# Short-convolution units regrouped between the chunks of a 31-tap convolution, with layer norm pieces and input statistics moved, in an eight-core Conformer block

## The reference

```
sh1, sc1, gt1, sh2, sc2, gt2 = split(silu(c) @ w_ada + b_ada, 6)
h = rmsnorm(x, norm1_g) * (1 + sc1) + sh1
p = h @ w_in                          # 2*512 + 3*512 + 2*1024 columns
# mixer A
u = (u_a + b) * sigmoid(u_b + b)
u = causal_dwconv(u, width 31) + conf_dw_b
u = silu(layernorm(u))
y_a = u @ conf_w_out + conf_b_out
# mixer B
v = g_b * causal_dwconv(g_c * v, width 3)
y_b = v @ sc_w_out
mixed = (sigmoid(g1) * y_a + sigmoid(g2) * y_b) @ w_o
x = x + gt1 * mixed
h2 = rmsnorm(x, norm2_g) * (1 + sc2) + sh2
x = x + gt2 * ((silu(h2 @ w_g) * (h2 @ w_u)) @ w_down)
out = rmsnorm(x, final_g)
```

## Time and profile before

| | us |
|---|---|
| median of 3 runs | 923.08 |
| the profiled execution | 923.02 |
| its span on core 2, the slowest | 921.5 |
| span of the other cores | 918.5 to 921.4 |
| TensorE busy | 874.9 |
| VectorE busy | 470.6 |
| ScalarE busy | 325.1 |
| POOL busy | 28.9 |

### The profile page before, as it was taken

One profiled execution on the slowest core, in us unless ns is written; L12 is line 12 of the kernel. 1 busy time (PEld: TensorE's weight loads), 2 busy tenths in 40 slices (PEclk: granted clock), 3 DMA queues, 4 the chain that ended last, 5 costly groups with the idle time before them and its releaser, 6 DMA issues.

```text
span 921.5 us, 13134 instructions; the slowest of 8 cores (918.5 to 921.5 us)
## 1 busy us (share of the span) xinstructions
PE 874.9 (95%) x4487; PEld 402.6 (44%) x4487; DVE 470.6 (51%) x741; ACT 325.1 (35%) x496; POOL 28.9 (3%) x58
## 2 busy tenths in 40 slices
PE   3698899899999999999999999999999999999995
PEld 0243344444444444444444444444444444444464
DVE  2767846666666666657742212472213532214677
ACT  4676776655522222237751111101110011112333
POOL 0000000000000000000110000000000000000000
PEclk9999999999999999999999999999999999999998
DMA  8995444671658736294008212231222222101225
GB/s 233 291 261 139 94 105 103 136 145 31 173 125 256 193 97 156 70 196 124 1 1 138 35 35 46 46 55 27 35 46 46 47 35 35 35 9 27 91 104 172
DMA packets 29155, 91.93 MB, mean 100 GB/s; under 512 B 3233, under 2 KB 13729, under 8 KB 24866
## 3 DMA queue, kind: packets, MB, share of 16 engines
q1 hardware_dynamic: 23618, 59.26, 21.8%
q0 software_dynamic: 5184, 31.57, 20.5%
q10 hardware_dynamic: 288, 0.26, 0.1%
HBM read 105.73 MB, written 8.39 MB: 124 GB/s over the span
## 4 chain that ended last, share of the span: by engine, by line
PE 82%; DVE 6%; ACT 4%; issue 3%; DMA 3%; SPq 1%; DVEq 0%; ACTq 0%
PE ps L363 62%; PE ps L1098 17%; DVE arena L345 4%; ACT arena L342 3%; DMA arena<-xc 2%; DVE arena L349 2%; PE ps L773 2%; PE ps L655 1%; SPq L413 1%; ACT L342 1%; PE ps L560 1%; PE ps L453 0%; DMA arena<-arena 0%; DVE arena L352 0%; DMA outT<-arena 0%
## 5 line engine op out<-in xcount | busy, mean ns | idle before, releaser
L363 PE MATMUL ps<-arena 128*128 128x512 bf16 (+1 forms) x3028 | 661.7, 380 | 10.8 <-DVE arena L345 5.1
L363 PEld LDWEIGHTS ps<-arena 128*128 128x128 bf16 (+1 forms) x3028 | 296.1, 98 | 370.5 <-issue 18.0
L345 DVE TENSOR_TENSOR arena<-ps,arena 128x512 bf16<-128x512 f32 (+2 forms) x158 | 108.1, 685 | 305.8 <-PE ps L363 221.9
L342 ACT ACTIVATE arena<-arena 128x512 bf16<-128x512 f32 (+3 forms) x233 | 149.6, 673 | 145.8 <-DVE arena L349 77.5
L342 ACT ACTIVATE arena<-ps 128x512 f32<-128x512 f32 x122 | 71.9, 594 | 303.4 <-PE ps L363 302.7
L349 DVE SCALAR_TENSOR_TENSOR arena<-ps,arena 128x512 f32<-128x512 f32 (+2 forms) x176 | 127.4, 725 | 69.7 <-PE ps L1098 41.1
L1098 PE MATMUL ps<-arena 128*128 128x512 bf16 (+1 forms) x800 | 154.0, 353 | 0.0
L345 DVE TENSOR_TENSOR arena<-arena 128x512 f32<-128x512 f32 (+5 forms) x211 | 125.7, 619 | 36.7 <-ACT arena L342 23.5
L342 ACT ACTIVATE arena<-ps,arena 128x512 f32<-128x512 f32 (+1 forms) x117 | 76.4, 686 | 122.3 <-PE ps L363 105.8
L1098 PEld LDWEIGHTS ps<-arena 128*128 128x128 bf16 x800 | 78.3, 98 | 74.2
L349 DVE SCALAR_TENSOR_TENSOR arena<-arena 128x512 f32<-128x512 f32 (+3 forms) x83 | 57.6, 703 | 21.5 <-ACT arena L342 17.4
(11 more groups left out here) (25 smaller groups left out, 33.8 us busy)
## 6 DMA issues: line engine op xcount, KB each, us to landing
arena<-wada SPq DMA_DIRECT2D x48, 512.0 KB, 7.8
arena<-w POOLq DMA_DIRECT2D x21, 1024.0 KB, 9.6
arena<-arena SPq DMA_DIRECT2D x64, 130.0 KB, 2.8
arena<-xc SPq DMA_DIRECT2D x8, 1024.0 KB, 8.2
arena<-xc SPq DMA_DIRECT2D x4, 2048.0 KB, 17.3
arena<-wd POOLq DMA_DIRECT2D x8, 768.0 KB, 6.9
outT<-arena SPq DMA_DIRECT2D x24, 256.0 KB, 2.9
arena<-w POOLq DMA_DIRECT2D x6, 512.0 KB, 11.5
```

Source lines behind the costliest of these rows:

```text
L342: sch.op("act", lambda e: e.activation(out=out, in_=in_, func=func, **kw), reads=reads, writes=writes)
L345: sch.op(eng, lambda e: e.tensor_tensor(out=out, in0=in0, in1=in1, op=op), reads=reads, writes=writes)
L363: fns.append(lambda e, lt=lt, rh=rh, i=i: e.matmul(bank[b], lhsT=lt, rhs=rh, start=(i == 0), stop=(i == n - 1)))
```

## The change

Six things are changed, all in `stages`:

1. `in_tmp(1, ·)` is called for two tiles each at k = 1, 2, 3 and 4, in place of four at k = 1 and four at k = 2.
2. `in_sq(2)` moves from behind unit (0,1) to behind unit (0,0). The hook with `in_red(2, 6)` and `in_apply(2)` moves from ahead of the third group of unit (1,0) to ahead of its second. `glu_raw(2, 0)` moves ahead of unit (1,0).
3. In `in_apply` the h tile k = 7 is written by VectorE and no longer by ScalarE.
4. In the u units after chunk 0 both `st_a` and `st_b` are issued behind u(1,3), and `st_j` for j = 0 and 1 behind u(2,3) and u(3,3).
5. Chunk 1 follows after unit (0,2). Between chunks 1 and 2, and between 2 and 3, there are four units, and three after chunk 3. The statistics and pieces fill the first three units after each chunk.
6. The empty piece before the layer norm of chunk 3 goes, and a function `warm` that nothing called.

```diff
-            def warm(n):
-                sch.pe_group([lambda e: e.matmul(bank[0][:, 0:416], lhsT=ones_d, rhs=cst, start=True, stop=True) for _ in range(n)],
-                             reads=[B_cst], writes=[B_bank[0]])
...
-                if k == 1:
-                    for kk in range(4):
-                        in_tmp(1, kk)
-                elif k == 2:
-                    for kk in range(4, KD):
-                        in_tmp(1, kk)
+                for kk in {1: (0, 1), 2: (2, 3), 3: (4, 5), 4: (6, 7)}.get(k, ()):
+                    in_tmp(1, kk)
...
                 for k in ks:
                     in_tmp(r, k)
-                    in_h(r, k, "act")
+                    in_h(r, k, "dve" if k == KD - 1 else "act")
 
             sc_unit(0, 0, (shift_cols, None))
+            in_sq(2, dve=(1, 3, 5, 7))
             glu_raw(0, 0)
             sc_unit(0, 1)
-            in_sq(2, dve=(1, 3, 5, 7))
             glu_raw(1, 0)
+            glu_raw(2, 0)
 
             def hook2():
                 in_red(2, 6)
                 in_apply(2)
-            sc_unit(1, 0, (None, hook2))
-            glu_raw(2, 0)
+            sc_unit(1, 0, (hook2, None))
             glu_raw(3, 0)
...
                 if j == 1:
+                    step()
                     sch.wait_tok("pool", tok_xsh)
                     load_slot("A", w8_d[4])
             sc_unit(0, 2)
-            sc_unit(0, 3)
             flush()
             tok_xsh = conv_a(1)
...
-            sc_unit(1, 2)
-            sc_unit(1, 3)
-            sc_unit(2, 0)
+            for (j, r) in ((0, 3), (1, 2), (1, 3), (2, 0)):
+                sc_unit(j, r)
             flush()
             tok_xsh = conv_a(2)
...
-            for r in range(1, NR):
-                sc_unit(2, r)
+            for (j, r) in ((2, 1), (2, 2), (2, 3), (3, 0)):
+                sc_unit(j, r)
             flush()
             load_slot("CWO", w4_d[0])
             conv_a(3)
-            pend.append(lambda: None)
             conv_b(3)
-            for r in range(NR):
+            for r in range(1, NR):
                 sc_unit(3, r)
             flush()
```

## The result

The changed kernel is slower: 931.21 us median against 923.7 us for the kernel before, measured beside it; ratio 1.0078, 95% interval 1.006 to 1.0097. Forecast were 926.0 us and a range up to 928.9. The direction was right, the size was not. The profiled execution took 928.94 us, the shortest of its runs. Some executions, of nearly every kernel here, are longer by up to 18% with a lower granted clock on one die or both (here 1039.05 us, clock 0.855 to 0.881 on cores 0 to 3): the ratios and their intervals leave them out, the medians do not, and without it the median of the changed kernel is 930.8.

A forecast was written before the change was run, and what follows sets the result against it. TensorE, busy 95% of the span, was taken as the bound, so order only moves its idle time. Core 7's span 921.2 - 1.8 + 4.0 + 1.2 = 924.6, plus 1.5 around it, said as 926.0 us; range 920.8 to 928.9.

The forecast's parts named there:

- -1.8 + 4.0 + 1.2: Forecast's sum on core 7: early parts with x2 late -1.8, later gate stage +4.0, clock fall +1.2 us.
- u phase and chunk 1: Layer norm pieces earlier: gcs(0,2) 5.7 us later; ahead of chunk 1's statistics TensorE idles 7.4 us in some four waits.
- Four units: Cycles between chunks: TensorE bounds them at 28.8 us each, and the bank wait of 2.59 us goes.
- Landing step: Statistics of x2: second half lands at 75 on the slowest core, so early parts give -1.8 us instead of -4.9.
- its 15.9 us: Statistics of x2: time from the landing of x2's second half to the last h2 tile.
- x1 pairs, -1.8: Streamed phase: TensorE's waits of 0.27 and 1.51 us both go; bounds nothing to -2.0 us.
- Clock term, +1.2: After the wait near 158 us the granted clock falls and slows the chunk: +1.2 us, bounds 0 and +1.7.
- From the profiled execution to the median: Last step to the time: 1.5 us around the profiled span, with the sum taken to stand against the median too.
- (a) cancel: Rival, whole kernel: x2 in time on every core, early gain and late stall cancel, 923.3 us; 26%.
- (b): Rival, whole kernel: early gain stays and added table loads are covered, -4.9 + 1.4, 919.5 us; 17%.
- Its sign, gcs(0,2) before 142.7: u phase: rival (b) decides if gcs(0,2) starts before 142.7 us.
- (c): Rival: x2 late and every table switch costs a second 1.28 us, +2.6, 928.6 us; 8%.

The follow-up runs named there:

- Experiments 1: Kernel before with one part of the change alone: x1 pairs, ratio 1.0005; statistics of x2, 0.9965; order of u phase and units, 1.0095.
- experiment 2: Changed kernel without the extra u-phase step: 923.76 us, ratio 1.0; or with pieces 0 and 1 both behind u(3,3), 24 loads: 926.5 us, 1.0011.
- experiments 2 and 4: The 4: kernel before with the statistics part and four units between chunks only once, after chunk 1: 924.23 us, ratio 0.9976.
- experiment 3: Changed kernel with 26 matmuls whose result nobody reads, ahead of chunk 1's statistics: 929.81 us, ratio 1.0051.
- third set: Statistics alone and pairs with statistics, both again, and each with x2 asked for at once, against the kernel before: ratios 0.9963, 0.9949, 0.9969, 0.9962 (x2-sooner: statistics, then both).

## Why the prediction was wrong

The steps that failed: the landing of x2 on the slowest core was taken too early (+1.0 us), the fall of the clock at the gate stage was left out (+1.7), and the way from the profiled execution to the median was put at nothing (+2.3). The stall ahead of chunk 1's statistics, the main cost, was forecast rightly.

By its own steps, on the slowest core: the forecast stands on core 7 of before, the measured values are core 6's. The forecast for the seventh gate group is core 7's own, 0.9 behind the end of its last wait (235.0), with -1.8 + 4.0 + 1.2; its measured value is the start of that group on core 6. The last column is what was missed since the row above.

| point | forecast | measured | missed here |
|---|---|---|---|
| chunk 0 starts | 109.8 | 110.8 | +1.0 |
| seventh gate group | 238.4 | 239.5 | +0.1 |
| end of span | 924.6 | 927.4 | +1.7 |
| profiled execution | 926.0 | 928.9 | +0.1 |
| median | 926.0 | 931.2 | +2.3 |

- **u phase and chunk 1: right.** With the 1.8 us taken off, the forecast had gcs(0,2) at 143.5, the last Silu at 150.1 and the product at 156.1, with 7.4 us of idle time. Measured: 143.54, 150.11, the statistics at 155.91, and 7.02 us in three waits. That the absolute times agree is luck: chunk 0 started 1.0 later than forecast, and ran at full clock, which gave it back. The mechanism holds without it: counted from the start of chunk 0, gcs(0,2) comes at 34.1 us on the two cores that ran chunk 0 at half clock, and at 28.4 on the three that did so in the kernel before, which is the 5.7 us of the forecast. Experiments 1 and 2 show the cause. The Trainium skill ("ScalarE: Activation LUTs", "Table sets: the hidden batching unit") says to group calls by set; experiment 2 shows what that is worth here, 6.3 us of the segment.
- **Four units: right in size, wrong in worth.** 176.81 to 205.5 is 28.7 us a cycle, the forecast 28.8, and the 2.59 went. But experiments 2 and 4 show the waits moving on: 5.4 us before, 5.4 with the new groups and the old loads. (The sum has 57.8 for two such cycles, which are 57.6.)
- **Landing step, "for the slowest core I take a landing at 75": too early.** It was 76.2, and chunk 0 started 0.8 us sooner than on core 7 before (0.3 sooner than on core 6 itself), not 1.8. The mechanism and its 15.9 us held; the mean core won 2.5.
- **x1 pairs, -1.8: half right.** The waits went, the stream closed up. Alone the pairs won nothing (ratio 1.0005), since I took the w_ada and slot landings as covered and they were next. Beside the statistics move, with x2 in time, chunk 0 came 1.5 us sooner, in one trace of each and with the clock of 0.81 in both.
- **Clock term, +1.2: mis-sized.** I priced one fall, by the 1.7 us that it cost chunk 0. It was 6.8 us behind the 7 us of waits, 2.4 us by experiment 3. On core 6 this hid behind two smaller errors (the waits 0.4 shorter; core 6 had no fall in chunk 0, where core 7 had one), so that the segment came out to 0.1. **And it was counted in one place only:** the last wait grew from 1.76 to 2.58 us, the clock fell there too, and behind the seventh gate group core 6 took 687.9 us where 686.2 were forecast, 1.7 more (1.3 more on the mean core). I had called the order after 234 us untouched and never asked what the new last wait would do to the clock.
- **From the profiled execution to the median, taken as nothing.** That held for the kernel before (923.02 against 923.08), where chunk 0 starts at 110.2 to 111.6 on all cores whatever x2 does. In the changed kernel it starts between 105.6 and 110.8, by landings that differ from execution to execution, and the time is that of the slowest of eight. The profiled execution was the shortest. In four of its executions core 4 took from 920.7 to 930.2 us and core 3 from 920.0 to 928.7; over nineteen of the kernel before no core varied by more than 4.4. By the median of 930.8 the 2.3 is 1.9. I draw the link to the landings from one profiled execution of each kernel; the landings of the others were not recorded.

Rivals: (a) cancel, fell, and would have fallen with x2 in time on every core: the early parts together are worth 4.7 us at best (0.9949) and the order costs 8.8. (b) fell: the loads were not covered. Its sign, gcs(0,2) before 142.7, did not show on core 6 (143.54); it did on five cores, but only because their chunk 0 was early, and from its start the time was 32.4 to 34.1 us on every core, against 27.3 to 28.4 before. (c), a second 1.28 us for each switch, was near in time (928.6) and false in mechanism: the load at 137.22 is followed by the sigmoid at 138.52, with nothing between. The Trainium skill ("ScalarE: Activation LUTs", section "What ACT_TABLE_LOAD costs") puts the drain at 1.38 us a switch; these rows do not show it.

The sizes of the three parts add up within the intervals: by the ratios, pairs 0.5 (within noise), statistics -3.2 and order +8.8 give +6.1, against 7.2 measured for all three.

## What to carry to other kernels

Moving work earlier across an activation-table boundary costs the loads and also the round of waiting that each boundary puts between two in-order queues: keep pieces that share a table adjacent, even if each then runs a little later. When a wait of a few microseconds appears on TensorE, price the granted clock behind it at every such wait, also one that merely grew. A regrouping that removes waits in one place may only move them: add up all of them before and after, and see whether one of them is now long enough for the clock to fall behind it. When an edit makes a start hang on a DMA landing, take the latest landing of eight cores over several executions, not that of one profile, and run the kernels to be compared in one set: an interval from one chip did not hold on the next. Before times of two sets are compared, look at the granted clock of both; before two stretches are compared, see that they hold the same matmuls.

## What was not expected of the hardware

One and the same kernel (pairs and statistics) had a ratio of 0.9988 (0.9978 to 0.9999) on one chip and 0.9949 (0.9936 to 0.9962) on another: intervals that do not touch. In one profiled execution of each, x2's second half landed 4.5 us later on the first of them; that it was the chip, and not the hour or the execution, is not shown.

Between 40 and 900 us the half clock came in stretches of 3.4 or 6.8 us. Ahead of the gate stage it went with the wait: it fell around the end of a wait of 2.5 to 2.9 us on 38 of 44 cores (six kernels) and around the end of one of 1.6 to 1.8 us on none of 68 (nine kernels). In the third set a third value, 0.81, stood between 42 and 69 us for 15.1 us on cores 4 to 7, in all four kernels and in no trace of the first two sets or of the two kernels of the change.
